# Attention of differences: the order in which the query blocks of a head are taken

## The reference, cut to what matters

```python
def diff_attention(q, k, v, lq1, lk1, lq2, lk2, subln_g, lam_init):
    # 4 heads; each has two maps with 64-wide q and k (rotary), and one 128-wide v
    ...
    def block(args):                       # one block of 128 queries
        q_blk, i = args
        s = jnp.einsum('bhmqd,bhmkd->bhmqk', q_blk, k).astype(jnp.float32) * scale
        qpos = i * Q_BLOCK + jnp.arange(Q_BLOCK)
        mask = kpos[None, :] <= qpos[:, None]
        p = jax.nn.softmax(jnp.where(mask, s, -jnp.inf), axis=-1)
        a = p[:, :, 0] - lam * p[:, :, 1]
        return jnp.einsum('bhqk,bhkd->bhqd', a.astype(v.dtype), v)
    ...
    o = rms_norm(o, subln_g) * (1.0 - lam_init)
```

## Time and profile before

| | |
|---|---|
| Runs of the kernel, us | 4422.3, 4429.48, 4454.76 (median 4429.48) |
| Profiled execution, us | 4451.4, of which 4449.6 are the span |
| PE busy | 4183.7 us, 94% of the span |
| PEld busy | 3346.5 us, 75% |
| DVE busy | 1957.9 us, 44% |
| ACT busy | 1384.3 us, 31% |
| POOL busy | 1417.9 us, 32% |
| mean granted TensorE clock | 0.958 of full speed |
| chain that ended last | PE 76%, DVE 14%, ACT 5% |

### The profile page before, as it was taken

The page is one execution under the profiler, slowest core; times in us unless marked ns, Lnnn a source line. Parts: engine busy times, 40 slices in busy tenths (PEclk is TensorE's granted clock), DMA queues, the critical chain, the costliest instruction groups (busy, mean ns, idle before and its releaser), DMA issues.

```text
span 4449.6 us, 50121 instructions
## 1 busy us (share of the span) xinstructions
PE 4183.7 (94%) x19671; PEld 3346.5 (75%) x19671; DVE 1957.9 (44%) x3435; ACT 1384.3 (31%) x2896; POOL 1417.9 (32%) x1449
## 2 busy tenths in 40 slices
PE   8999999789999998998888999998998988999998
PEld 4677788677888877885576888887884576888887
DVE  2231313382777765216734343445315734334444
ACT  1121212122666662214533221223214533221122
POOL 1313121181333325322134443342422133443441
PEclk9999999799999999997898999999997898999999
DMA  5312110332000003110022111113110022111112
GB/s 181 98 46 74 51 52 31 101 112 55 9 10 8 8 14 105 55 36 1 1 97 80 49 53 48 43 57 105 56 31 8 1 88 82 57 48 44 52 53 97
DMA packets 224534, 244.60 MB, mean 55 GB/s; under 512 B 43861, under 2 KB 165221, under 8 KB 224297
## 3 DMA queue, kind: packets, MB, share of 16 engines
q1 hardware_dynamic: 190456, 162.81, 12.4%
q10 hardware_dynamic: 33840, 78.58, 5.2%
HBM read 209.11 MB, written 30.08 MB: 54 GB/s over the span
## 4 chain that ended last, share of the span: by engine, by line
PE 76%; DVE 14%; ACT 5%; issue 2%; POOL 1%; DMA 1%; SPq 0%; ACTq 0%; DVEq 0%; POOLq 0%
PE ps L127 73%; PE ps L130 4%; DVE cst_sm L150 3%; DVE ml_p L139 2%; ACT thi L133 1%; DVE tlo L139 1%; DVE tfi L147 1%; DVE m_hb L147 1%; ACT m_junk L133 1%; ACT tfi L133 0%; POOL mix_z L139 0%; ACT ml_o L133 0%; ACT f_ta L133 0%; DVE m_z L147 0%; DVE m_z L139 0%
## 5 line engine op out<-in xcount | busy, mean ns | idle before, releaser
L136 POOL CAST whi<-wst 128x512 fp32r<-128x512 f32 (+3 forms) x538 | 378.2, 703 | 2065.8 <-DMA wst<-in_w_down 539.3
L139 POOL TENSOR_TENSOR wlo<-wst,whi 128x512 fp32r<-128x512 f32 (+3 forms) x538 | 704.6, 1310 | 43.2
L127 PE MATMUL ps<-thi,whi 128*128 128x512 f32 x1760 | 690.4, 392 | 8.6 <-POOL wlo L139 5.7
L127 PE MATMUL ps<-tlo,whi 128*128 128x512 f32 x1760 | 688.8, 391 | 0.0
L127 PE MATMUL ps<-thi,wlo 128*128 128x512 f32 x1760 | 688.5, 391 | 0.0
L127 PE MATMUL ps<-whi,thi 128*128 128x512 f32 (+3 forms) x1560 | 605.1, 388 | 6.0 <-DVE mix_z L139 2.6
L127 PE MATMUL ps<-wlo,thi 128*128 128x512 f32 (+3 forms) x1560 | 593.2, 380 | 0.0
L127 PE MATMUL ps<-whi,tlo 128*128 128x512 f32 (+3 forms) x1560 | 592.9, 380 | 0.0
L147 DVE SCALAR_TENSOR_TENSOR f_ta<-f_ua,tfi,f_ta 128x1024 f32<-128x1024 f32 x88 | 122.0, 1386 | 735.4 <-ACT f_ta L133 733.8
L127 PEld LDWEIGHTS ps<-thi,whi 128*128 128x128 f32 x1760 | 333.4, 189 | 79.7 <-POOL wlo L139 6.9
L127 PEld LDWEIGHTS ps<-thi,wlo 128*128 128x128 f32 x1760 | 332.9, 189 | 69.8
(11 more groups left out here) (299 smaller groups left out, 6659.9 us busy)
## 6 DMA issues: line engine op xcount, KB each, us to landing
wst<-in_w_up SPq DMA_DIRECT2D x704, 64.0 KB, 2.0
wst<-in_w_down SPq DMA_DIRECT2D x88, 256.0 KB, 2.6
wst<-in_w_in SPq DMA_DIRECT2D x64, 256.0 KB, 2.7
wst<-in_a_w_in SPq DMA_DIRECT2D x72, 192.0 KB, 2.4
wst<-in_ada_w SPq DMA_DIRECT2D x48, 256.0 KB, 3.4
tfi<-in_ada_w SPq DMA_DIRECT2D x48, 256.0 KB, 2.7
wst<-in_w_out SPq DMA_DIRECT2D x32, 256.0 KB, 5.4
m_xr<-scr_x ACTq DMA_DIRECT2D x16, 512.0 KB, 3.6
```

What stands on the lines that cost most here:

```text
L127: return self.none if self.e is None else self.e.matmul(*a, **k)
L136: return self.none if self.e is None else self.e.tensor_copy(*a)
L139: return self.none if self.e is None else self.e.tensor_tensor(*a)
```

## The change

The order of the eight query blocks within each head is another; the heads keep their order. All three engines' programs are generated from the same list, so the buffers, the waits and the places of retention and window steps are set by position as before, while the widths at each position differ. The last block of a head is 3 in place of 0.

```diff
-    UNITS = [(h, j) for h in range(4) for j in range(7, -1, -1)]
+    UNITS = [(h, j) for h in range(4) for j in (7, 0, 6, 1, 5, 2, 4, 3)]
```

## The result

| | before | after |
|---|---|---|
| median of 20 runs, us | 4431.9 (4422.2 to 4454.8) | 4457.0 (4448.4 to 4481.7) |
| ratio | | 1.0049, 95% interval 1.0036 to 1.0062 |
| profiled execution: time, span, us | 4451.4, 4449.6 | 4454.7, 4452.9 |
| PE busy, us | 4183.7 | 4172.7 |
| mean granted clock | 0.958 | 0.959 |

The new order is slower by about 22 us by the ratio (the medians differ by 25). That is less than the 1% (44 us) which the prediction took as about what a measurement can tell, but the interval is clear of 1. The two profiled executions differ by 3.3 us only. So the pair of traces alone would mislead; a second profile of the kernel before was needed.

The account below looks back on a forecast made before the run. TensorE was taken as the bound in the mean of the second-block attention stage; idle of 0.6 + 0 + 2.8 + 4.0 = +7.4 us a layer, clock 0, made +15 on 4429.5: 4444 us, range 4406 to 4478.

Parts of the forecast that it names:

- The signs that the prediction named: Profile marks: third-head idle near 6.6 us, fourth near 14, waits at 17 and 25, changed low-clock stretches, stage 242 to 244.
- its own test: Wrong if third-head idle is no more than 3.9 us, or low-clock total moves from 85 us by more than 10.
- The third head, +2.8: Positions 16 to 23: idle TensorE 6.65 us against 3.9, from waits of 2.25, 2.5 and 1.9.
- the lateness of VectorE: Positions 21 to 23: scores(21) start 1.0 us late after VectorE's retention, mix and late maximum; waits sum to 1.9.
- The first and second heads, +0.6 and 0: Idle TensorE a layer: first head 5.1 us for 4.5, second 6.2 for 6.5, taken as 0.
- The fourth head, +4.0 of idle: Positions 25 to 31: longer waits at 25, 28 and 28 to 31, together +4.0 us a layer.
- The wait of position 28: Old wait of 4.31 us, behind eight scalings and eight retention normalisations, grows by 1.0.
- The waits at 28 to 31: Value products wait for the hi/lo split of two retention tiles behind larger blocks: +1.9 us.
- The last two mixes: Blocks 4 and 3 on VectorE might each meet a GpSimd weight split, 0.62 us; taken as 0, at most 1.2 a layer.
- The clock, 0: Low-clock stretches: first -1.7 us, that at 2180.5 -1.7, third head's +3.4, sum 0; bounds -12 and +14.
- The slower rival: Clock falls in new gaps at 17, 19 to 21 and 25: +14 us more a layer, 4472 us; chance 0.22.
- The faster rival: Even pairs win: added waits cancel, stretches at 2146.4 and 2180.5 vanish, -12 us a layer, 4405; chance 0.2.

Follow-up runs that it names:

- Retention late: New order with the step for two retention tiles at positions 28 to 31 moved to the end of the round, against the kernel before: ratio 1.0007.
- the spread: Eight scalings of heads 0 to 2 issued one a round; against the kernel before, new order 0.9991, or 0.9981 with the retention tiles moved late as well.
- heavy-last order: Heads 0 to 2 descending, last head in the order 3, 2, 1, 0, 7, 6, 5, 4, against the kernel before: ratio 1.0071.
- old order with the retention tiles late: Kernel before with only the retention tile step at positions 28 to 31 moved to the end of the round: ratio 0.9979.

## Why the prediction came out as it did

**Direction and size.** Forecast +15 us, measured +21.7 (0.0049 of 4432) with 16 to 28 as interval. The time of 4444 was 13 us short and within the range. The forecast was +7.4 us of idle TensorE time a layer and nothing from the clock. Measured in the pair of traces, idle time grew by 10.0 and 9.4 us a layer, by head in layer 0 +1.3, +1.5, +0.4 and +6.8, where +0.6, 0, +2.8 and +4.0 were forecast. The sum comes near because errors of both signs partly cancel.

**The signs that the prediction named.** The waits at position 17 and before the transposes at 25 came, and the shorter first low stretch (17.1). Idle time of the third head was 4.3 (near 6.6 forecast). That of the fourth, to the drain of the values as in the prediction, was 17.0 (near 14 forecast, 10.1 before), and the stage to there 236.9 (242 to 244 forecast). The low stretch behind position 19 was 6.8, not longer. The low-clock total went from 85.3 to 71.7 us in layer 0 and to 68.3 in layer 1, by more than the 10 that the prediction itself called its being wrong. So it was right about the time and the sign, and wrong by its own test about the clock.

**Luck.** Against the trace from which it was drawn, the new order made the stages only 0.9 and 0.2 us longer, not 7.4. The cost shows against executions that this trace did not stand for, those with a short second head. That the forecast of the total came near is therefore in part luck.

**The third head, +2.8: failed.** At position 17 the waits are 0.72 and 0.82, forecast 0.9, 0.7 and 0.65: the third did not come. At position 20 the wait is 2.32, forecast 2.5 over three places. The 1.9 of positions 21 to 23 did not come at all (0.25). Idle in the head is 50.42 - 46.11 = 4.3, against 3.9. It is 1.7 us longer in both layers, 1.3 of it busy time; the low clock there is 10.2 us for 6.8. The failed step is the lateness of VectorE that I carried from position to position: before the maximum of position 21 VectorE waited 1.38 us for TensorE. TensorE was at half clock for 6.8 us just before; how much of the lateness that covered was not separated.

**The first and second heads, +0.6 and 0: too low.** Position 11's wait is 4.61, forecast 5.05, old 4.56. But at position 9, where 0.65 in all was forecast, TensorE waits 1.11 and 0.67 for the two exponentials, and idle time in the second head is 8.0 for 6.5. In the first it is 11.7 for 10.4. The first low stretch is 17.1, as forecast, for 20.5, and the first head is 1.1 us shorter, not longer.

**The fourth head, +4.0 of idle: right place, too small, by partly other terms.** Against the kernel before idle grew by 6.8; against the same work in the old order by 3.8, and the head by 9.8 and 10.3 us. Terms: the transposes of position 25 wait 2.54 (forecast 2.6, right). Those of position 27 wait 1.26 for a ScalarE copy behind the load of the square root table, which I had not laid out. The wait of position 28 is 8.73, forecast 5.3: the term that was sized worst. Position 28 itself starts no later (31.4 us after the head's first scores, 34.5 before); VectorE's chain of 2.19 us of scalings and 5.94 of retention normalisations sets it, and TensorE has less to do ahead of it. Two things take that cover away. One is the small blocks: with the new order in the last head alone the wait is 7.36, though 17.1 us of half clock lie ahead of it as before. The other is the clock: with the new order ahead and the old one in the last head it is 7.57, with 3.4 us of half clock there. The rows of that chain after:

```profile
2186.93 2.19 DVE L147 SCALAR_TENSOR_TENSOR tfi<-tfi,tfl 128x128 f32<-128x128 f32 x8
...
2189.42 5.94 DVE L139 TENSOR_TENSOR c_rn<-c_rn,cst_va 128x256 f32<-128x256 f32 x8
```

The waits at 28 to 31 grew by 0.6 (4.47 for 3.84), forecast 1.9. The last two mixes met no weight split: they took 0.89 and 0.75 us, as mixes of these widths did before (0.88 and 0.75), so the 0 for that term was right.

**The clock, 0: failed.** By how much depends on what the last head is held against. With the same work in the old order, as many as 6.0 and 7.6 us of the 9.8 and 10.3 are slow clock: 40.9 us at 1.2 GHz for 23.9 in layer 0. Against the kernel before, the last head has only 4 us more of it (40.9 for 36.7), since the 17.1 us from 2180.5 are gone, and the second head has 19 us less (10.3 for 29.7), against that trace's long kind. The slower rival priced half the length of stretches behind added gaps, but put them at 17, 19 to 21 and 25 with +14 a layer; the added ones came at positions 29 to 31, where large blocks now meet waits of 0.8 to 1.7 us (0.4 to 1.3 before). The faster rival's time, 4405, is out. Of its two stretches the one at 2146.4 has its counterpart at 2143.3 of the same 6.8, and the one at 2180.5 did vanish.

**The base.** I gave the time from the median but drew waits and clock from one execution whose both layers were of the long kind. This was not harmless: the clock term of 0 was taken against more slow clock than a typical execution seems to have, and the second head's gain, 7.5 us in that trace, is none against the other kind.

**Open.** What holds the clock low in the last head is not isolated. Retention late brought most of it back alone (clock 0.85), but with the spread as well it was at 0.71 and 0.82 in the two layers profiled. In the heavy-last order the clock fell among small blocks and stayed low through large ones. No run took the waits away entirely, or changed the sizes without moving the waits. Whether size or wait decides was not tried.

## What to carry to other kernels

Where work of falling size is replaced by alternating size, price each stage by what else fills it: here the order cost nothing that the times show in three heads and about 10 us a layer in the last, where retention's products had ended (that their absence is the reason is likely, but was not tried). Compare orders by the length of a stretch with the same instructions, not by idle sums, since slow work hides waits. And take a second profile of the kernel before: one trace can be a specimen 20 us from the median.

## What was unexpected of the hardware

The same instructions in the same layer stage took 249.4 or 238.1 us in one execution, and most of it is clock in the second head (0.77 or 0.92). Behind a wait of 2.6 us at the end of the first head in both layers the clock stayed low for 13.7 us or for 3.4.

And ahead of a point that VectorE sets, half clock costs little. In the old order with the retention tiles late, the two layers of one execution have the same 97 TensorE instructions between the last head's first scores and position 28. At a clock of 0.72 TensorE is busy 28.6 us and then waits 4.39; at 0.90 it is busy 22.2 and waits 7.99:

```profile
2146.27:2180.74 34.47, 28.55 (x97) 16.94 (x96) 24.57 (x53) 14.73 (x36) 7.03 (x9) 0.72 0.00 0
3484.49:3516.23 31.74, 22.22 (x97) 13.52 (x96) 24.53 (x53) 14.73 (x36) 7.01 (x9) 0.90 0.00 1
```

So 6.3 us more of busy time made position 28 only 2.7 us later. Half the length of a low stretch was only an upper bound of its price here.
